# Moving the rotary sum to VectorE and the doubling of the keys to ScalarE in a hybrid attention and retention layer

## The reference

```python
h = rmsnorm(x, norm_mix_pre)
qa, ka, va, qr, kr, vr, gr = split(h @ w_in)            # seven groups of 512 columns, 8 heads of 64
ya = moba_attention(qa, ka, va, rel_bias)               # softmax attention with a relative bias
yr = retention(qr, kr, vr, gr)                          # qr and kr go through rotary() first
x = x + rmsnorm(concat(ya, yr) @ w_out, norm_mix_post)
u = causal_conv3(rmsnorm(x, norm_ffn_pre) @ w_up);  f = gelu(u_gate) * u_val
x = x + rmsnorm(f @ w_down, norm_ffn_post)

def rotary(x):                                          # x1, x2: low and high half of a head's 64 columns
    return concatenate([x1 * cos - x2 * sin, x1 * sin + x2 * cos])
```

## Time and profile before

| | |
|---|---|
| median of 3 runs | 658.28 us (658.04 to 659.0) |
| profiled execution, its time | 657.82 us |
| profiled execution, its span | 656.0 us |
| granted TensorE clock, mean | 0.999 |
| busy, TensorE | 637.3 us (97%) |
| busy, VectorE | 384.0 us (59%) |
| busy, ScalarE | 299.4 us (46%) |
| busy, GpSimd | 69.1 us (11%) |

### The profile page before, as it was taken

How to read it: one execution, slowest core, us unless ns; L and a number is a source line. 1 busy time by engine, 2 the same in 40 slices (tenths; PEclk the granted TensorE clock), 3 DMA queues, 4 the chain that set the end, 5 groups by cost and what they waited for, 6 DMA issues and landing times.

```text
span 656.0 us, 9379 instructions
## 1 busy us (share of the span) xinstructions
PE 637.3 (97%) x3210; PEld 526.6 (80%) x3210; DVE 384.0 (59%) x565; ACT 299.4 (46%) x485; POOL 69.1 (11%) x88
## 2 busy tenths in 40 slices
PE   7999999999999899999999999999999999999996
PEld 7887877777787687899888888888888888878885
DVE  3448548646854975985755555555555654463455
ACT  5548327526733854664433333333333433362351
POOL 5402102111210302420000000000000000000002
PEclk9999999999999999999999999999999999999999
DMA  9634223331412145641433333333333023422323
GB/s 282 189 119 128 66 64 97 96 96 32 145 47 89 72 160 161 193 129 65 129 96 96 96 96 96 96 96 96 96 95 100 29 95 97 160 64 61 96 68 128
DMA packets 87110, 69.15 MB, mean 105 GB/s; under 512 B 2265, under 2 KB 76169, under 8 KB 87090
## 3 DMA queue, kind: packets, MB, share of 16 engines
q1 hardware_dynamic: 85618, 63.62, 32.2%
q0 software_dynamic: 1472, 5.26, 2.5%
HBM read 66.76 MB, written 2.12 MB: 105 GB/s over the span
## 4 chain that ended last, share of the span: by engine, by line
PE 83%; DVE 8%; ACT 3%; issue 3%; DMA 1%; POOL 1%; DVEq 0%; SPq 0%; POOLq 0%; ACTq 0%
PE bank L435 77%; PE bank L515 1%; DVE work L1165 1%; ACT work L827 1%; DMA raw<-in_w_in_dram 1%; DVE work L1174 1%; DVE ws L1048 1%; PE bank L578 1%; DVE yT L1094 1%; DVE work L1183 1%; PE bank L506 1%; DVE work L1184 1%; PE bank L505 1%; PE bank L446 1%; POOL ws L360 1%
## 5 line engine op out<-in xcount | busy, mean ns | idle before, releaser
L435 PE MATMUL bank<-hT,ws 128*128 128x512 f32 (+1 forms) x1872 | 412.4, 376 | 5.7 <-DVE work L1183 4.3
L435 PEld LDWEIGHTS bank<-hT,ws 128*128 128x128 f32 x1872 | 327.9, 188 | 67.1 <-issue 6.7
L435 PE MATMUL bank<-ws,yT 128*128 128x512 f32 x720 | 166.7, 390 | 0.3 <-PE bank L435 0.3
L435 PEld LDWEIGHTS bank<-ws,yT 128*128 128x128 f32 x720 | 134.3, 188 | 28.4 <-issue 1.1
L1048 DVE TENSOR_TENSOR ws<-raw,ws 128x1024 fp32r<-128x1024 f32 x85 | 103.5, 1218 | 6.9 <-ACT ws L768 6.4
L768 ACT ACTIVATE ws<-raw 128x1024 fp32r<-128x1024 f32 x88 | 92.5, 1052 | 15.5 <-PE bank L435 11.7
L1327 DVE TENSOR_TENSOR ws<-raw,ws 128x1024 fp32r<-128x1024 f32 x22 | 26.9, 1224 | 51.2 <-ACT ws L1008 51.2
L985 ACT ACTIVATE gains<-bank,conv 128x512 f32<-128x512 f32 x22 | 17.1, 779 | 75.0 <-PE bank L435 75.0
L1008 ACT ACTIVATE ws<-raw 128x1024 fp32r<-128x1024 f32 x22 | 23.3, 1057 | 56.2 <-PE bank L435 56.2
L985 ACT ACTIVATE rot<-bank,conv 128x512 f32<-128x512 f32 x22 | 17.1, 779 | 67.7 <-PE bank L435 67.7
L1304 DVE SCALAR_TENSOR_TENSOR gains<-bank,conv,gains 128x511 f32<-128x511 f32 x22 | 16.5, 750 | 52.8 <-ACT gains L985 52.8
(11 more groups left out here) (111 smaller groups left out, 477.4 us busy)
## 6 DMA issues: line engine op xcount, KB each, us to landing
raw<-in_w_up_dram SPq DMA_DIRECT2D x44, 512.0 KB, 3.8
raw<-in_w_in_dram SPq DMA_DIRECT2D x28, 512.0 KB, 4.4
raw<-in_w_down_dram SPq DMA_DIRECT2D x22, 512.0 KB, 3.9
raw<-in_w_out_dram SPq DMA_DIRECT2D x16, 512.0 KB, 3.6
xs<-in_x_dram SPq DMA_DIRECT2D x4, 512.0 KB, 6.4
work<-bias_vectors POOLq DMA_DIRECT2D x4, 512.0 KB, 3.9
work<-in_decay_dram POOLq DMA_DIRECT2D x4, 512.0 KB, 4.5
out_dram<-work SPq DMA_DIRECT2D x4, 256.0 KB, 2.0
```

The lines of the kernel that those rows point to most:

```text
L435: return nc.tensor.matmul(dst, st, mv, start=start, stop=stop)
```

## The change

The sum of the two products is made by VectorE, right behind them, with waits for both. The doubled high part of the keys is written by ScalarE, straight from the source of the stack (the PSUM bank, or `rotc`) and ahead of the copy to the own half, in both stacks of keys; the signal stays on the last copy. `double_keys`, `rotary_sum`, their two semaphores and TensorE's waits for them go. GpSimd keeps the two table loads of a turn and the small square roots.

```diff
-        aq_double, rq_double = sem("aq_double"), sem("rq_double")
...
-            def rotary_sum(i, side):
-                pool.wait_ge(sin_done, 2 * i + side + 1)
-                nc.gpsimd.tensor_tensor(rotc, rotc, rots, ALU.add).then_inc(rotated, 1)
-
-            def double_keys(keys, hi, signal, i):
-                pool.wait_ge(hi, 2 * i + 1)
-                for h in range(2):
-                    own, other = slice(HD * h, HD * h + HD), slice(HD * (1 - h), HD * (1 - h) + HD)
-                    nc.gpsimd.tensor_copy(keys[other, h, :], keys[own, h, :]).then_inc(signal, 1)
-                    pool.wait_ge(signal, 2 * i + h + 1)
...
                 pool.dma_start(btab, window(bias_dram, 2 * i, 2)).then_inc(btab_loaded, 16)
-                double_keys(ksA, aq_hi, aq_double, i)
...
                 if i:
                     group_rstd(i - 1)
-                rotary_sum(i, 0)
-                double_keys(ksR, rq_hi, rq_double, i)
-                rotary_sum(i, 1)
...
-                    pe.wait_ge(rq_double, 2 * k + 2)
...
-                    pe.wait_ge(aq_double, 2 * i + 2)
...
             def stack_hi(src, keys, queries, side, signal):
                 for h in range(2):
-                    own = slice(HD * h, HD * h + HD)
+                    own, other = slice(HD * h, HD * h + HD), slice(HD * (1 - h), HD * (1 - h) + HD)
                     if side == 0:
+                        nc.scalar.activation(keys[other, h, ::-1], src[own, :], ACT.Copy)
                         ins = nc.scalar.activation(keys[own, h, ::-1], src[own, :], ACT.Copy)
...
                 nc.vector.tensor_tensor(rotc, bank[UNIT_BANK[j]][:], rot[:, 0, :], ALU.mult).then_inc(cos_done, 1)
                 nc.vector.tensor_tensor(rots, rots, rot[:, 1, :], ALU.mult).then_inc(sin_done, 1)
+                dve.wait_ge(cos_done, 2 * i + side + 1)
+                dve.wait_ge(sin_done, 2 * i + side + 1)
+                nc.vector.tensor_tensor(rotc, rotc, rots, ALU.add).then_inc(rotated, 1)
```

## The result

The changed kernel takes 661.33 us (median of 6 runs, 661.02 to 661.87) against 658.64 us for the kernel before (median of 6, 657.79 to 659.37): ratio 1.0047, 95% interval 1.0036 to 1.0058. The forecast was 660.6 us, 2.4 us slower; it is 2.7 us slower. Three of the six runs of before took 657.8 to 658.3 us and three 659.0 to 659.4: against the lower three the change costs 3.3 us, so the 2.7 holds some chance.

What follows compares the result with a forecast made beforehand. TensorE, busy 637.3 of 656.0 us, was taken as the bound, so only its waits count. Terms 1.15 + 0.52 + 3 x 0.23 = 2.36 us gave a median of 660.6 us, range 658.9 to 662.3 (8 in 10), own range 659.5 to 661.6.

Steps and rivals of the forecast that it cites:

- (a): Start of turn 0: four key copies on ScalarE delay VectorE's low part, so TensorE starts unit 2 1.15 us later.
- (b): Attention keys in turns 1 to 3: 1.20 us of extra copies stay covered by VectorE's decay work; cost 0.
- (c): Steps u=4 and 5, turns 1 to 3: 1.43 us wait stays; VectorE's work behind scaling 4, and exp 5, 0.34 earlier.
- (d): Steps u=5 to 7: key stack 1.25 us longer, ScalarE 0.91 later; VectorE's low part ends within 0.1 of before.
- (e): Steps u=7 to 9: TensorE gets block 7 0.23 us later in each of turns 1 to 3, 0.52 in turn 0.
- The collision: VectorE's scaling beside GpSimd's rotary sum: without it, 1.06 us shorter at 384 columns and 1.12 at 512.
- 1 (faster, if the copies hide): Further copies hide under ScalarE's waits and only the collision counts: 656.7 us with nothing added; chance 0.06.
- 2 (the chain comes out at nothing): Only the start of turn 0 costs, steps u=5 to 9 nothing: 1.0 to 1.2 us, giving 659.4; chance 0.17.
- 3 (the scaling stays slow, GpSimd's table load): Something else, for instance GpSimd's earlier table load, holds VectorE's scaling: clearly slower, about 667 us; chance 0.05.
- 4 (VectorE's new wait reaches TensorE by a weight split): VectorE's wait for the stack delays its weight splits and TensorE meets one: 1 us a turn, 663 to 665; chance 0.05.

Runs made afterwards that it cites:

- the last experiment but one: Changed kernel with the two copies of each head in the other order, own half first, doubled half second; 661.83 us, ratio 1.0045.

## Why the prediction was right, point by point

**What bounds the kernel.** Right: all of the difference between the two profiles lies in TensorE's waits of the mixer, and the rest of the span is the same to 0.02 us.

**(a) The start of turn 0**, 1.15 us forecast: TensorE's new wait is 1.24 us, the stretch behind the start of the stack is 1.19 us longer, and putting those copies elsewhere gave 1.21 of it back (11.44 to 10.23).

**(b) The attention's keys in turns 1 to 3**, 0: right. With their doubling moved, turn 1 stays at 56.51.

**(c) The wait of 1.43 us stays and the work behind it comes 0.34 earlier.** The wait is 1.42. From TensorE's start of step u=6 to exp 5 in turn 1 it is now 2.89 us (105.93 to 108.82) and was 3.15 (104.16 to 107.31), so 0.26 and not 0.34 was gained.

**(d) The stack.** Taken at 1.25 us more, it is 1.42: from exp 5 to probsT 4 it went from 1.89 us to 3.31 (112.13 - 108.82). The copies stand about 0.64 apart and not 0.625, and the first starts 0.12 later; with the own half first, in the last experiment but one, it does not. This is the term that was mis-sized most. VectorE's low part was to end within 0.1 us of before; counted from step u=6 it ends 7.60 us in (113.53) where it ended 7.25 in (111.41), 0.35 later. That moves the gate product, and with it comes TensorE's new wait of 0.42 us, which the prediction did not foresee.

**(e) The end of the chain.** The sum was put at 0.72 us; from the start of the sine product to the reciprocal behind the sum it is 1.40 (116.52 to 117.92) where it was 0.60, so it costs 0.80: it starts 0.11 after the end of the sine product (117.20 to 117.31), where 0.04 was assumed. With these terms, 0.08 in (c), 0.17 in (d) and 0.08 here, the forecast of 0.23 becomes the measured 0.56 in turn 1 (turns 2 and 3: 0.55 and 0.53); the 0.52 of turn 0 becomes 0.80. The prices add up to 1.2 + 0.8 + 3 x 0.55 = 3.7 us; the spans differ by 3.4, as the runs differ by 0.2 before the change is reached.

**How much was luck.** The places and the signs were right, but every term between (c) and (e) was off the same way, and the prices come to 1.3 us more than the forecast's 2.36. The two profiled executions show that: 657.82 was to become 660.2 and became 661.23. That the medians differ by 2.7, close to the forecast, owes something to the three slower executions of before. The prediction's own range, 659.5 to 661.6, does not come out of its bounds either: with every bound at its low end the terms add 0.64 us, with every one at its high end 3.03, which gives 658.9 to 661.3.

**The collision** was worth what was forecast: the scalings take 0.42 and 0.49 us now, 1.47 and 1.58 again beside GpSimd's add, and 1.12 and 1.24 beside its memset. The rule of the Trainium skill in SBUF — State Buffer, "Who interferes with whom", has a VectorE instruction in a two-port mode and GpSimd shut each other out. The trace agrees as far as VectorE was held by both the add and the memset. It does not bear out the rule's order, by which the one that issues first keeps the ports: the scaling is recorded 0.03 us ahead of the add and 0.01 ahead of the memset, and it is the scaling that was held, while the add took 1.26 us, about what the sum took before (1.29).

**Rivals.** 1 (faster, if the copies hide) describes what happens when they are moved off the stack. It did not happen in the change since they do not hide there. 2 (the chain comes out at nothing) was wrong: it came out at 0.56 us a turn. 3 (the scaling stays slow, GpSimd's table load) did not occur: the load is now issued at 115.15, ahead of the scaling at 118.11. Whether the load by itself can hold a scaling was not tried. 4 (VectorE's new wait reaches TensorE by a weight split) was wrong in its place, but not wholly in kind: the wait at (d) does reach TensorE, through the gate product, 0.42 us at 115.60. It adds nothing to the price, as block 7 is later still.

## What to carry to other kernels

The two halves of the change pulled in opposite directions, 2.7 us gained and 5.6 lost when made alone, so try the halves apart before a joint verdict. Ask of a moved instruction not how busy its new engine is but what stands behind it and who waits for that: the same copies cost nothing where ScalarE was idle and 5 us in front of a signal and a swap. Work whose result is wanted a turn later needs a signal of its own, not the one of the work that is wanted next. And an engine's listed waits are not all that a fix can win: in turn 0 the sum's move gave 0.54 us where the list had 0.34.

## What was not expected of the hardware

**After some waits of TensorE its clock falls, and that costs again.** In the run with GpSimd's add, TensorE waits 2.94 us in turn 0, and then runs below full clock. Windows of that profile (the third figure from the end is the granted clock):

```profile
62.00:65.00 3.00, 0.17 (x2) 0.18 (x3) 2.86 (x5) 1.61 (x4) 1.48 (x2) 1.00 0.02 5
65.00:68.00 3.00, 3.00 (x12) 2.21 (x11) 1.12 (x2) 2.44 (x5) 0.51 (x1) 0.66 0.56 156
68.00:71.00 3.00, 3.00 (x31) 2.50 (x31) 2.38 (x3) 1.22 (x2) 0.00 (x0) 0.77 0.65 193
71.00:74.00 3.00, 3.00 (x14) 2.44 (x14) 1.38 (x3) 0.81 (x2) 0.00 (x0) 1.00 0.61 175
```

A mean of 0.66 and 0.77 over two windows is a part of each at 1.2 GHz and the rest at 2.4. From block 7's transposes to the retention values it took 9.45 us (64.83 to 74.28) where the changed kernel took 7.89 (62.16 to 70.05): another 1.56 us behind the wait.

The length of the wait alone does not tell whether this happens. In turn 1 of the same run a wait of 2.06 us is followed by 7.90 us for the same stretch, nothing lost. In turn 3 a wait of the same 2.06 us is followed by 7.62 us (242.31 to 249.93) where the changed kernel took 6.06 (231.62 to 237.68), 1.56 lost again, with these windows:

```profile
240.00:246.00 6.00, 3.94 (x16) 2.64 (x16) 4.68 (x7) 4.57 (x8) 1.26 (x1) 0.79 0.15 47
246.00:250.00 4.00, 4.00 (x37) 3.43 (x36) 2.56 (x3) 0.91 (x2) 0.00 (x0) 0.89 0.43 151
```

**The start of the kernel differs from run to run, and by the same clock.** TensorE waits there for the first normed rows. In the profiled executions this wait was 2.00 us before, 1.19 after and 2.60 with only the doubling, and the clock stayed at 1.00 behind all three. It was 1.93 with the attention's keys doubled later, and there the clock was 0.50 from 11 to 13 us. With the own half first the wait was 3.00 and the clock 0.50 from 10 to 16 us. The stack of the keys, which starts at 27.06 us in the changed kernel, started at 28.82 and 30.01 in these two. These two executions took 1.8 and 2.4 us more than the shortest of the same kernels (662.08 against 660.25, 663.11 against 660.73), so the start is the likely reason; it is not shown, as only one execution of each kernel has a profile. The difference is about as large as the price of the change, and a reason to compare stretches rather than spans. What makes the first wait long or short was not tried.

**ScalarE has an order effect of its own:** 0.12 us at each end of the stack in the experiment with the own half first. The same half of the partitions written by two neighbours is not enough for the shorter start. In the changed kernel the copies at 110.19 and 110.83 both write the lower half and stand 0.64 apart like the others, but they read different halves. And the swap, whose first copy writes partitions 0 to 31 from 32 to 63, starts 0.21 us after the record of exp's sum, as the stack does there (113.28 to 113.49, 109.34 to 109.55), where the stack with the own half first starts 0.09 after it (112.02 to 112.11). All of these rows fit a rule that a copy starts early only where neither the first partition that it reads nor the first that it writes differs from the instruction in front. No run tried it apart.
